# Page numbers read once per sample pair, and another order inside the sample steps of a decoder attention stage

## What is computed

```
past = cache_kv[i][page_table].reshape(n_dec, past_len, N_KV_SLOTS, N_KV, HEAD_DIM)
win = jnp.concatenate([state_win[i], jnp.stack([kw, vw], axis=2)], axis=1)
s_s = jnp.einsum('bqgrd,bgqkd->bqgrk', q, kg) * scale
p_s = _masked_probs(s_s, mask_s[:, :, :, None, :])
o_s = jnp.einsum('bqgrk,bgqkd->bqgrd', p_s.astype(vg.dtype), vg)
return gates[..., 0:1] * o_c + gates[..., 1:2] * o_s + gates[..., 2:3] * o_w
```

## Time and profile before

| | us |
|---|---|
| median of 3 runs | 2693.15 (2690.9 to 2693.22) |
| the profiled execution's own time | 2692.34 |
| its span (first to last instruction) | 2690.6 |
| TensorE busy (matmuls) | 2481.0 |
| VectorE busy | 1265.4 |
| ScalarE busy | 969.6 |
| GpSimd busy | 193.9 |

### The profile page before, as it was taken

The page is one execution under the profiler, slowest core; times in us unless marked ns, Lnnn a source line. Parts: engine busy times, 40 slices in busy tenths (PEclk is TensorE's granted clock), DMA queues, the critical chain, the costliest instruction groups (busy, mean ns, idle before and its releaser), DMA issues.

```text
span 2690.6 us, 46761 instructions
## 1 busy us (share of the span) xinstructions
PE 2481.0 (92%) x18309; PEld 2153.3 (80%) x18309; DVE 1265.4 (47%) x2416; ACT 969.6 (36%) x2011; POOL 193.9 (7%) x333
## 2 busy tenths in 40 slices
PE   5999999989999878889989999999899988888997
PEld 4999999987788544469979999999877864445896
DVE  4444232545544655564364432236355556555535
ACT  4222122234444344442332222222444434444222
POOL 0000000000000213220000000000000002322000
PEclk9999999989989899989989999999798999999898
DMA  5333343414210323373233425432321212333621
GB/s 173 135 125 110 95 154 115 135 37 136 69 42 23 95 68 100 98 217 101 79 139 130 141 83 136 136 111 80 125 77 40 63 51 76 98 96 114 189 95 42
DMA packets 267745, 277.53 MB, mean 103 GB/s; under 512 B 59352, under 2 KB 256280, under 8 KB 266118
## 3 DMA queue, kind: packets, MB, share of 16 engines
q1 hardware_dynamic: 263398, 238.81, 29.4%
q0 software_dynamic: 4128, 35.74, 3.6%
HBM read 247.60 MB, written 43.53 MB: 108 GB/s over the span
## 4 chain that ended last, share of the span: by engine, by line
PE 75%; DVE 8%; SPq 7%; ACT 4%; issue 3%; DMA 1%; DVEq 1%; POOL 1%; ACTq 0%
PE ps L710 39%; PE ps L863 12%; PE ps L808 11%; SPq L515 4%; SPq L496 3%; DVE chL L1782 2%; ACT chH L1411 2%; PE ps L838 2%; PE ps L1096 2%; PE ps L888 1%; PE ps L965 1%; DMA k_win<-in_state_win 1%; PE ps L989 1%; PE ps L998 1%; PE ps L950 1%
## 5 line engine op out<-in xcount | busy, mean ns | idle before, releaser
L388 DVE TENSOR_TENSOR wL<-w_raw,wH 128x2048 fp32r<-128x2048 f32 (+2 forms) x112 | 253.3, 2262 | 432.3 <-ACT wH L379 427.3
L710 PE MATMUL ps<-hH,wH 128*128 128x272 f32 x1792 | 373.6, 290 | 17.3 <-DVE hL L1634 17.2
L710 PE MATMUL ps<-hH,wL 128*128 128x272 f32 x1792 | 374.2, 290 | 0.0
L710 PE MATMUL ps<-hL,wH 128*128 128x272 f32 x1792 | 371.7, 289 | 0.0
L1782 DVE TENSOR_TENSOR chL<-ps,chH 64x256 fp32r<-64x256 f32 x512 | 216.6, 423 | 230.2 <-ACT chH L1411 223.0
L710 PEld LDWEIGHTS ps<-hH,wH 128*128 128x128 f32 x1792 | 283.7, 189 | 20.7 <-issue 16.3
L1411 ACT ACTIVATE chH<-ps 64x256 fp32r<-64x256 f32 x512 | 206.4, 403 | 252.2 <-PE ps L863 246.2
L710 PEld LDWEIGHTS ps<-hL,wH 128*128 128x128 f32 x1792 | 282.9, 189 | 0.0
L710 PEld LDWEIGHTS ps<-hH,wL 128*128 128x128 f32 x1792 | 282.8, 190 | 0.0
L863 PE MATMUL ps<-chH,w1H 128*128 128x504 f32 (+1 forms) x640 | 260.1, 406 | 15.1 <-DVE chL L1773 15.1
L863 PE MATMUL ps<-chL,w1H 128*128 128x504 f32 (+1 forms) x640 | 252.1, 394 | 0.0
(11 more groups left out here) (288 smaller groups left out, 3931.7 us busy)
## 6 DMA issues: line engine op xcount, KB each, us to landing
w_raw<-in_w_in SPq DMA_DIRECT2D x68, 1024.0 KB
craw<-in_cache_kv SPq DMA_DIRECT2D x256, 128.0 KB, 3.3
k_sel<-in_cache_kv SPq DMA_DIRECT2D x128, 128.0 KB, 3.4
v_sel<-in_cache_kv SPq DMA_DIRECT2D x128, 128.0 KB, 3.4
out_new_win_sample<-in_state_win POOLq DMA_DIRECT2D x16, 1016.0 KB, 5.8
w_raw<-in_w_out_a SPq DMA_DIRECT2D x8, 1024.0 KB
w_raw<-in_w_in SPq DMA_DIRECT2D x32, 256.0 KB
k_win<-in_state_win SPq DMA_DIRECT2D x16, 512.0 KB, 4.6
```

Source lines behind the costliest of these rows:

```text
L388: dve.tensor_tensor(block_part(wL, b), block_part(w_raw, b), block_part(wH, b).bitcast(F32), ALU.subtract).then_inc(w_lo, 1)
L710: last = nc.tensor.matmul(ps[:, bank + hf, 0:HALF], st, x[:, k, hf * HALF:(hf + 1) * HALF], start=k == 0 and w is wH and x is xH, stop=k = ...
```

## The change

- `page_numbers` reads the 16 page numbers of a pair into registers; `page_rows` takes one of them. In `load_pages` they are read ahead of a wait on `c_tp` that moves into the function. In the attention stage they are read once for keys and values of a pair, ahead of the wait on `sa_kt`; per pair the loop then issues the keys, waits for `s_fin`, and issues the values.
- TensorE's `sample_step` begins with two key jobs; scores, key jobs and output parts stand in another order; `sample_out` has four parts and writes to bank Y instead of 1; the third group of scores goes to bank 1 instead of Y.
- ScalarE and VectorE copy keys in another order. `combine_pair` and the second bias of a pair move from VectorE's step to unit k = 2, `turn_back` from k = 2 to k = 4, `copy_turned` from k = 4 to k = 5.

The diff, where lines that only put `bank` for `1` are left out and the indent is cut:

```diff
@@ -491,28 +491,36 @@
-def page_rows(l, seq, j, first, n):
-
-    page = sp.value_load(pages[0:1, ds(seq * NPAGE + j, 1)], min_val=0, max_val=a["cache_kv"].shape[1] - 1)
-    return a["cache_kv"][ds(l, 1), ds(page, 1), :, first:first + n].rearrange("l o (c t) s g d -> c (l o t) (s g d)", t=HC)
+def page_numbers(pair):
+
+    return [sp.value_load(pages[0:1, ds(2 * pair * NPAGE + j, 1)], min_val=0, max_val=a["cache_kv"].shape[1] - 1)
+            for j in range(2 * NPAGE)]
+
+def page_rows(l, page, slot):
+
+    return a["cache_kv"][ds(l, 1), ds(page, 1), :, slot:slot + 1].rearrange("l o (c t) s g d -> c (l o t) (s g d)", t=HC)
...
     slot, kv = sample_unit(n) % 2, n // 5
+    numbers = page_numbers(n % 5 - 1)
+    if n in (3, 4, 6, 7, 8, 9):
+        before = {3: 1, 4: 2, 6: 3, 7: 4, 8: 6, 9: 7}[n]
+        sp.wait_ge(c_tp, TP_N * l + tps(before) + 8)
     for s in range(2):
         for j in range(NPAGE):
-            src = page_rows(l, 2 * (n % 5) - 2 + s, j, kv, 1)
+            src = page_rows(l, numbers[NPAGE * s + j], kv)
             sp.dma_start(craw[slot][16 * j:16 * j + 16, s], src).then_inc(c_in[slot], 16)
...
-def load_half(l, pair, slot, sel, win, done):
+def load_half(l, pair, numbers, slot, sel, win, done):
...
         for j in range(NPAGE):
-            sp.dma_start(sel[16 * j:16 * j + 16, s], page_rows(l, 2 * pair + s, j, slot, 1)).then_inc(done, 16)
+            sp.dma_start(sel[16 * j:16 * j + 16, s], page_rows(l, numbers[NPAGE * s + j], slot)).then_inc(done, 16)
         src = a["state_win"][l, 2 * pair + s].rearrange("(p k) s g d -> p k s (g d)", k=4)
@@ -566,23 +574,21 @@
     load_w1(l, "cmp_w1_v")
-    for n, before in ((3, 1), (4, 2), (6, 3), (7, 4), (8, 6), (9, 7)):
-        sp.wait_ge(c_tp, TP_N * l + tps(before) + 8)
+    for n in (3, 4, 6, 7, 8, 9):
         load_pages(l, n)
+    numbers = page_numbers(0)
     sp.wait_ge(c_tp, TP_N * l + TP_N)
...
     sp.wait_ge(c_mm, nth(c_mm, 40 * l + 40))
-    load_half(l, 0, 2, k_sel, k_win, s_k)
-    load_half(l, 0, 3, v_sel, v_win, s_v)
+    load_half(l, 0, numbers, 2, k_sel, k_win, s_k)
+    load_half(l, 0, numbers, 3, v_sel, v_win, s_v)
     for pair in range(1, 4):
-        if pair > 1:
-            sp.wait_ge(s_fin, 4 * l + pair - 1)
-            load_half(l, pair - 1, 3, v_sel, v_win, s_v)
+        numbers = page_numbers(pair)
         sp.wait_ge(sa_kt, 48 * l + 12 * pair)
-        load_half(l, pair, 2, k_sel, k_win, s_k)
-    sp.wait_ge(s_fin, 4 * l + 3)
-    load_half(l, 3, 3, v_sel, v_win, s_v)
+        load_half(l, pair, numbers, 2, k_sel, k_win, s_k)
+        sp.wait_ge(s_fin, 4 * l + pair)
+        load_half(l, pair, numbers, 3, v_sel, v_win, s_v)
@@ -1055,7 +1061,7 @@
-    def sample_out(pair, part):
+    def sample_out(pair, part, bank):
@@ -1064,20 +1070,21 @@
...
         if part < 2:
...
                 for n, s, gp, rows in strips:
...
+        else:
+            for t in (2 * part - 4, 2 * part - 3):
+                for n, s, gp, rows in strips:
+                    nc.tensor.matmul(ps[rows, bank, 2 * P:3 * P], spT[:, 8 + t, rows], v_win[:, s, t, gp * P:(gp + 1) * P], start=t == 0, stop=False)
         if part == 1:
             for n, s, gp, rows in strips:
...
-        if part == 2:
-            for t in range(4):
-                for n, s, gp, rows in strips:
-                    nc.tensor.matmul(ps[rows, 1, 2 * P:3 * P], spT[:, 8 + t, rows], v_win[:, s, t, gp * P:(gp + 1) * P], start=t == 0, stop=False)
...
+        if part == 3:
             for n, s, gp, rows in strips:
...
@@ -1108,6 +1115,9 @@
         X, Y = 6 + m % 2, 6 + (m + 1) % 2
+        if front is not None:
+            key_tp(front, 0, m)
+            key_tp(front, 1, m)
         pe.wait_ge(pa_ta, UNITS * l + 8 * m + 1)
@@ -1115,52 +1125,47 @@
         if front is not None:
-            key_tp(front, 0, m)
+            key_tp(front, 2, m)
+        pe.wait_ge(pa_o, 8 * l + m)
         if back is not None:
...
             probs_back(back, 2, X)
-            pe.wait_ge(pa_o, 8 * l + m)
             probs_back(back, 3, Y)
         if front is not None:
-            for k in (1, 2, 3):
+            for k in (3, 4, 5):
                 key_tp(front, k, m)
...
             sample_scores(front, 0, X)
-            key_tp(front, 4, m)
-            key_tp(front, 5, m)
         if back is not None:
-            pe.wait_ge(pa_exp, UNITS * l + 8 * m + 3)
-            sample_out(back, 0)
+            sample_out(back, 0, Y)
         if front is not None:
...
             key_tp(front, 7, m)
-            sample_scores(front, 1, 4)
         if back is not None:
-            sample_out(back, 1)
+            sample_out(back, 1, Y)
         if front is not None:
             key_tp(front, 8, m)
+            sample_scores(front, 1, 4)
             key_tp(front, 9, m)
+            key_tp(front, 10, m)
         if back is not None:
-            sample_out(back, 2)
+            sample_out(back, 2, Y)
         if front is not None:
-            key_tp(front, 10, m)
             key_tp(front, 11, m)
-            if back is not None:
-                pe.wait_ge(sa_te[1], 2 * it + 2)
-            else:
-                pe.wait_ge(pa_o, 8 * l + m)
-            sample_scores(front, 2, Y)
+        if back is not None:
+            sample_out(back, 3, Y)
+        if front is not None:
+            pe.wait_ge(pa_exp, UNITS * l + 8 * m + 3)
+            sample_scores(front, 2, 1)
...
-        pair, front = sample_block(m)
-        if front is not None:
-            pe.wait_ge(sa_se, 3 * (4 * l + front) + 3)
+        pair = sample_block(m)[0]
         pe.wait_ge(sa_y, 4 * l + pair + 1)
-        nc.tensor.transpose(ps[:, 6 + (m + 1) % 2, 0:P], sy[:], ident).then_inc(sa_yt, 1)
+        nc.tensor.transpose(ps[:, 6 + (m + 1) % 2, 3 * P:4 * P], sy[:], ident).then_inc(sa_yt, 1)
@@ -1170,8 +1175,7 @@
             copied(front, 11)
-        if k == 2 and back is not None:
-            pe.wait_ge(sa_y, 4 * l + back + 1)
+            pe.wait_ge(sa_se, 3 * (4 * l + front) + 3)
         if i + 2 < UNITS:
@@ -1190,7 +1194,7 @@
             sample_step(mm)
-        if k == 2 and back is not None:
+        if k == 4 and back is not None:
             turn_back(mm)
@@ -1510,14 +1514,16 @@
+        if front is not None:
+            key_in(0)
         if back is not None:
...
         if front is not None:
-            key_in(0)
+            key_in(2)
         if back is not None:
...
         if front is not None:
-            for k in (2, 3, 5, 6, 8, 9, 11):
+            for k in (3, 5, 6, 8, 9, 11):
                 key_in(k)
@@ -1963,7 +1969,7 @@
-    def combine_pair(pair):
+    def combine_pair(pair, bank):
@@ -1974,10 +1980,10 @@
         dve.wait_ge(sa_yt, 4 * l + pair)
...
         for n in (1, 2):
             dve.drain()
...
@@ -1988,7 +1994,7 @@
                 rows = slice(64 * g, 64 * g + 64)
-                src = ps[rows, 6 + (m + 1) % 2, 0:P].rearrange("p (s g t r) -> p g r s t", s=2, g=4, t=TS)[:, 2 * gp + g]
+                src = ps[rows, 6 + (m + 1) % 2, 3 * P:4 * P].rearrange("p (s g t r) -> p g r s t", s=2, g=4, t=TS)[:, 2 * gp + g]
                 dst = yT[rows, 4 * gp:4 * gp + 4, SEQ + 8 * pair:SEQ + 8 * pair + 8].rearrange("p r (s t) -> p r s t", s=2)
@@ -2010,12 +2016,8 @@
-        def bias(br, s):
-            c = 72 + 2 * (front % 2) + br
-            dve.tensor_reduce(out=small[:, c:c + 1], in_=s[:], op=ALU.max, axis=AX.X, negate=True)
-            dve.drain()
-            dve.tensor_scalar(small[:, c:c + 1], small[:, c:c + 1], SCALE, None, ALU.mult).then_inc(sa_m, 1)
-
+        if front is not None:
+            key_in(1)
         if back is not None:
@@ -2024,7 +2026,6 @@
         if front is not None:
-            key_in(1)
             key_in(4)
@@ -2033,24 +2034,31 @@
             dve.drain()
-            bias(0, ssel)
-        if back is not None:
-            combine_pair(back)
-        if front is not None:
+            sample_bias(front, 0, ssel)
             dve.wait_ge(sa_s, 3 * (4 * l + front) + 3)
-            dve.tensor_tensor(swsc[:, 0:WIN], ps[:, Y, :], C("wmask"), ALU.add).then_inc(sa_se, 1)
-            dve.drain()
-            bias(1, swsc)
+            dve.tensor_tensor(swsc[:, 0:WIN], ps[:, 1, :], C("wmask"), ALU.add).then_inc(sa_se, 1)
+
+    def sample_bias(pair, br, s):
+
+        c = 72 + 2 * (pair % 2) + br
+        dve.tensor_reduce(out=small[:, c:c + 1], in_=s[:], op=ALU.max, axis=AX.X, negate=True)
+        dve.drain()
+        dve.tensor_scalar(small[:, c:c + 1], small[:, c:c + 1], SCALE, None, ALU.mult).then_inc(sa_m, 1)
...
         mm, k = divmod(i, 8)
+        back, front = sample_block(mm)
         if i:
...
             turned(i - 1)
-        if k == 1 and sample_block(mm) != (None, None):
+        if k == 1 and (back, front) != (None, None):
             sample_step(mm)
+        if k == 2 and front is not None:
+            sample_bias(front, 1, swsc)
         if i + 2 < UNITS:
             maxima(i + 2)
+        if k == 2 and back is not None:
```

(24 more changed lines are left out.)

## The result

The change makes the kernel faster: median 2649.97 us (2640.2 to 2652.48, 4 runs) against 2693.18 us (2690.9 to 2693.94, 4 runs) before. The ratio is 0.9834, 95% interval 0.9807 to 0.9861: 43 us, where 47 were forecast. The profiled execution of the changed kernel took 2652.48 us (span 2650.7), 39.9 us less than that of before.

A forecast was written before the change was run, and what follows sets the result against it. TensorE, waiting for SyncE's issue of key transfers, bounds the kernel. -47.8 (steps) + 2.4 (unit 2) + 2.0 (m = 7) - 1.2 (m = 1) - 2.4 (clock) = -47.0 gives 2646 us, range 2638 to 2668.

The forecast's parts named there:

- The queue: SyncE, attention stage: numbers read once per pair in 9.1 us, each half issued in 13.6 us instead of 22.8.
- The landing: Last window transfer of the keys, DMA engines at some 0.8: landing stays near 4.3 us.
- 2.4 us of margin: Keys land 40.6 us after `s_fin`, 2.4 us ahead of TensorE's first key turn.
- rival 2: Keys still late at m = 4 and 6, reads or landings 5 us longer: 16 us more, 2662; chance 0.13.
- first sign: In the after profile, no wait of TensorE's key transposes (L1096) for `k_win`.
- The step: Each of six full sample steps: 14.9 us work plus 1.0 us waits, 15.9 us; gain 47.8 us in all.
- Rival 1: Copies of turned keys bound the sample step, only the key wait goes: 14 us more, 2660; chance 0.10.
- The wait at unit 2: Behind each full step TensorE waits 2.1 us for VectorE's copy; unit starts 0.4 us later, 2.4 us in all.
- The dear end: Upper bound behind each full step, 1.5 us each: the unit 2 wait with a clock drop behind it.
- The low clock: Two stretches of units at clock 0.93 lose their low clock, 1.2 us each: gain 2.4 us.
- m = 7: Behind the last step of each layer, the moved combination delays unit 2's output: 1.0 us each, 2.0 us given back.
- Rivals 3 and 4: SyncE issue stays 1.34 us, slower, about 2733, chance 0.04; waits move within the chain, no effect, 2692, chance 0.03.

The follow-up runs named there:

- e3: The changed kernel with each page of selected keys and values written into 128 partitions instead of 16; 2651.37 us, ratio 0.9837.
- e1: The kernel before with SyncE's part alone: page numbers read once per pair and the new queue order, other engines as before; 2657.6 us.
- e7: e6 with the combination behind m = 7 moved to unit 1 and its turn back to unit 3; 2639.01 us.
- e5: The changed kernel with `combine_pair` in unit 4, `turn_back` in unit 6, its copy in unit 7 of m = 2, 4, 6; 2645.31 us.
- e10: The changed kernel with the next pair's keys issued ahead of values and the late combination, transfers still into 16 partitions; 2646.06 us.
- e6: The changed kernel with page transfers into 128 partitions, keys issued ahead of values, and the late combination; 2643.65 us.
- e11: e6 run again, unchanged, in a later group; 2643.8 us.
- e2: The changed kernel with SyncE's part of the kernel before, a number read for every page; 2696.76 us, ratio 1.0004.
- e8: The changed kernel run again without edits; 2652.91 us.

## Why the prediction was right, and where it was off

- **The queue: right.** Reads, issue and order did what the steps said, 22.75 us against 22.7 and 13.6 against 13.6. A read took 0.54 us where I took 0.57; one slow issue among the values, of 1.33 us, made up for it.
- **The landing: mis-sized, and it is the term that failed.** "So the engines would be at some 0.8, and the landing should stay near 4.3" took the capacity of 293 GB/s from transfers of another shape. It was 8.11 us, and up to 9.22 at the other three places. 2.4 us of margin less 3.9 us of landing is 1.5 us late, and 1.10 was measured at m = 4. Against steps of 15.4 us, the late keys cost 8.0 us, waits and low clock behind them together. The evidence stood in my own row: 139 GB/s at a share of 0.49 is 284 GB/s at full share only if the share is work done, and for these transfers it was not. This is the part of rival 2 that held: it put 5 us on reads or landings. It was in force at the four places named, with 3.8 to 4.9 us rather than 5, and cost those 8.0 us rather than 16. The forecast's own first sign, no wait for `k_win`, did not come: there were 7.1 us of it. e3 shows the shape of the transfer as the cause. A rule fits by which it could work: the Trainium skill (SBUF — State Buffer, Door 1: The DMA port swizzle) says that DMA bandwidth depends on how many of 16 ports the partitions reach, and by its table 16 adjacent partitions reach 4. No view here shows ports, and the rates above are of pages into several groups of 16 partitions with windows into 128 among them, so they test no figure of that page; that part stays its word.
- **The step: right, a little better.** 15.4 us without a key wait, forecast 15.9; six of them made 3.1 us that hid a part of the landing's cost. That the total came within 4 us of the forecast owes something to this. Rival 1 falls: the copies do not bound the step.
- **The wait at unit 2: right in place and size** (2.06 us, forecast 2.1), and wrong in what it costs. At full clock the units take 41.8 us as before, where 0.4 us more each was forecast. "The dear end would be that wait with a clock drop behind it" is what came in 2 of 6 places of the changed kernel's profile, and in 22 of 36 over all profiles.
- **The low clock: half wrong.** I booked a gain of 2.4 us because the long key waits vanish. The two places had cost 0.8 and 1.1 us: the 23.0 us were held against a window of 21.8 us of another stretch, and a full stretch behind m = 6 is 22.3 us at full clock. One of them recovered (m = 6 in layer 0, 23.1 to 22.0 us), the other stayed low (42.9 and 42.8), and behind m = 6 in layer 1 a new one fell (22.3 to 22.9). In sum nothing changed (0.1 us), and I had 0 in sum; but that is luck. e1 shows that the premise was wrong: it has no key wait, and three low stretches.
- **m = 7: right in kind, too small**: 3.9 us given back, forecast 2.0. 1.2 us of it are low clock behind m = 7 of layer 1 (25.2 us to the end, 24.0 in layer 0). e7 gets a part of it again.
- **Rivals 3 and 4** fall with the issue interval of 0.76 us and with e1.

What stays open: why the same wait brings the clock down at one place and not at the next. And the medians say less than the profiles: e5 (keys late, combination late) and e10 (keys first, combination late) have nearly one median, 2645.3 and 2646.1, in two groups of runs, while the profiled stages of e10 are 7 us shorter. But the profile of e5 is its slowest execution, 9.4 us above its median, so the two can't be held against each other. How far the rest of the span moves by itself shows in e6 and e11, one kernel: from step m = 1 to the end of the attention stage their profiles agree to 0.4 us, and everything else took 2245.0 us in the one and 2252.8 in the other. A spread of 5 to 12 us within the runs of a kernel hides differences of 2 to 4 us, and I do not settle them.

## What to carry to other kernels

Take the speed of a transfer from a row with the same shape at a full share, not from the best rate in the profile: "0.49 busy at 139 GB/s" need not mean that twice the rate is to be had. When two engines race for one deadline, speeding up the one that is ahead yields nothing (e2: 0 us) until the other is faster (e1: 37 us, both: 43). And when an edit removes a wait and the time stays, look at the clock of the stretch behind the next-longest wait, and at how much the part of the span that you did not touch moved.

## What the runs showed of the hardware that I had not expected

- Page transfers of 128 KB into 16 partitions, issued every 0.76 us, ran at 146 to 152 GB/s with the DMA engines 0.92 to 1.00 busy, and a page landed after 5.5 us; issued every 1.34 us, the same pages ran at 139 GB/s at 0.49 and landed after 3.4 us. Into 128 partitions (e3) the window above has 218 GB/s at 0.72, and a page lands after 2.7 us.
- Eight such pages into 16 partitions took SyncE 6.27 us to issue, into 128 partitions 4.45 us.
- A standstill of TensorE of 2.06 us was followed by the lower clock level in 22 of 36 places, one of 1.46 us in 5 of 12, one of 1.36 us in 5 of 20, one of 1.01 us with one of 0.54 us some 8 us later in 0 of 30. The two levels show in one kernel as 0.65 and 1.12 us for the same four matmuls.
- Within one kernel the time follows the mean granted clock: the slowest and the fastest run of e8 are 9.5 us apart at 0.957 and 0.962.
